# Where a SwiGLU's row scale is multiplied in: on GpSimd onto the gate, or on VectorE onto the up result

## What is computed

```
for l in range(DEPTH):                       # DEPTH = 2
    h = rmsnorm(x, norm_mix[l])
    ... = split(h @ w_in[l])                 # S5, attention, retention -> mix
    x = x + mix @ w_out[l]
    h = rmsnorm(x, norm_ffn[l])              # x * rsqrt(mean(x*x) + eps) * g
    gate, up = split(h @ w_ffn_in[l], 2)     # 2 x 2816 columns
    x = x + (silu(gate) * up) @ w_ffn_out[l]
out = rmsnorm(x, norm_final)
```

## Time and profile before

| what | value |
|---|---|
| median of 3 runs | 2808.41 us (2803.58 to 2812.27) |
| profiled execution: time, span | 2810.1 us, 2808.3 us |
| busy time: PE / DVE / ACT / POOL | 2604.0 / 1568.6 / 1012.6 / 1308.5 us |
| share of the span | 93% / 56% / 36% / 47% |
| mean granted PE clock | 0.963 of full speed |

### The profile page before, as it was taken

How to read it: one execution, slowest core, us unless ns; L and a number is a source line. 1 busy time by engine, 2 the same in 40 slices (tenths; PEclk the granted TensorE clock), 3 DMA queues, 4 the chain that set the end, 5 groups by cost and what they waited for, 6 DMA issues and landing times. The chain is left out here.

```text
span 2808.3 us, 34676 instructions
## 1 busy us (share of the span) xinstructions
PE 2604.0 (93%) x13483; PEld 2058.0 (73%) x13483; DVE 1568.6 (56%) x2785; ACT 1012.6 (36%) x1486; POOL 1308.5 (47%) x818
## 2 busy tenths in 40 slices
PE   7898788989999998899999999988999999999999
PEld 5676555768777786677777777667777777788887
DVE  3858666778999225755231267376898952221112
ACT  5222143424343533232444432342443344322222
POOL 3332143435454474354554442443555446555655
PEclk9989898999999999999999999999999999999999
DMA  5232112212222144222232241221222223433332
GB/s 148 77 120 57 31 31 83 71 57 72 72 78 72 49 154 112 71 68 83 83 89 77 78 134 55 68 60 49 79 76 68 68 61 123 140 91 107 107 109 90
DMA packets 385665, 232.90 MB, mean 83 GB/s; under 512 B 29592, under 2 KB 371552, under 8 KB 383072
## 3 DMA queue, kind: packets, MB, share of 16 engines
q1 hardware_dynamic: 385136, 229.62, 27.6%
q10 hardware_dynamic: 368, 1.08, 0.1%
HBM read 213.88 MB, written 14.69 MB: 81 GB/s over the span
## 5 line engine op out<-in xcount | busy, mean ns | idle before, releaser
L678 POOL TENSOR_TENSOR w_lo<-w_raw,w_hi 128x1024 fp32r<-128x1024 f32 (+2 forms) x408 | 896.2, 2197 | 1353.0 <-ACT w_hi L789 1352.9
L1680 PE MATMUL psum<-h_hi,w_hi 128*128 128x512 f32 x1984 | 804.3, 405 | 32.1 <-POOL w_lo L678 20.3
L789 ACT ACTIVATE w_hi<-w_raw 128x1024 fp32r<-128x1024 f32 (+2 forms) x408 | 397.3, 974 | 1118.3 <-PE psum L1680 1062.3
L1680 PE MATMUL psum<-h_hi,w_lo 128*128 128x512 f32 x1984 | 782.8, 395 | 0.0
L1680 PE MATMUL psum<-h_lo,w_hi 128*128 128x512 f32 x1984 | 769.2, 394 | 0.9 <-POOL h_lo L686 0.9
L1680 PEld LDWEIGHTS psum<-h_hi,w_hi 128*128 128x128 f32 x1984 | 379.7, 191 | 147.2 <-issue 31.2
L1680 PEld LDWEIGHTS psum<-h_hi,w_lo 128*128 128x128 f32 x1984 | 378.6, 191 | 80.7
L1680 PEld LDWEIGHTS psum<-h_lo,w_hi 128*128 128x128 f32 x1984 | 378.9, 191 | 80.0 <-issue 2.5
L1309 DVE MAX8 top<-scores 128x8 f32<-128x512 f32 (+5 forms) x384 | 342.0, 891 | 7.6
L1311 DVE MATCH_REPLACE8 scores<-top,scores 128x512 f32<-128x512 f32 (+5 forms) x384 | 336.3, 876 | 0.0
L1680 PE MATMUL psum<-a_hi,w_hi 128*128 128x512 f32 x704 | 284.8, 404 | 12.4 <-POOL w_lo L678 7.7
(11 more groups left out here) (287 smaller groups left out, 2964.6 us busy)
## 6 DMA issues: line engine op xcount, KB each, us to landing
w_raw<-in_w_ffn_in_dram SPq DMA_DIRECT2D x176, 512.0 KB, 3.8
w_raw<-in_w_ffn_out_dram SPq DMA_DIRECT2D x96, 384.0 KB, 3.5
w_raw<-in_w_in_dram SPq DMA_DIRECT2D x68, 512.0 KB, 3.7
w_raw<-in_w_out_dram SPq DMA_DIRECT2D x32, 512.0 KB, 4.2
x_half<-xs SPq DMA_DIRECT2D x8, 1024.0 KB, 7.1
xs<-x_half SPq DMA_DIRECT2D x8, 1024.0 KB, 7.0
w_raw<-in_w_ffn_out_dram SPq DMA_DIRECT2D x32, 256.0 KB, 2.7
out_dram<-mixed SPq DMA_DIRECT2D x8, 512.0 KB, 3.7
```

Source lines behind the costliest of these rows:

```text
L678: eng.tensor_tensor(w_lo(u, n), w_raw[:, u % 3, 0:n], w_hi[:, u % 2, 0:n].bitcast(F32), ALU.subtract).then_inc(sems["weights_ready"], 1)
L789: act(w_hi[:, u % 2, 0:n], w_raw[:, u % 3, 0:n], ACTF.Copy).then_inc(sems["hi_ready"], 1)
L1680: return eng.matmul(out_, lhsT, rhs, start=start, stop=stop, skip_group_check=True)
```

## The change

On GpSimd the multiplication of `gate` by `row` is gone. On VectorE the eviction of an up bank in a deferred feed-forward becomes two multiplications: the bank times `row` into `atmp`, then `atmp` times `gate` in place. The PSUM bank is free for the next unit after the first one (semaphore `up_scaled`), and the second waits for the first and for the SiLU. The product is the same; the order of its factors is another. The non-deferred feed-forward (0,1) only takes its two waits in another order.

```
@@ gpsimd
                     if kind == "ffn" and i:
                         did, c, f = FFN[i - 1]
-                        if did == "gate" and deferred(kind, l, h):
-                            eng.wait_ge(sems["gate_ready"], st.add("gate_ready"))
-                            eng.tensor_tensor(gate, gate, row, ALU.mult).then_inc(sems["gate_scaled"], 1)
-                        elif did == "gate":
-                            st.add("gate_ready")
@@ vector
                 elif did == "up":
                     eng.wait_ge(sems["unit_done"], u)
-                    st.add("gate_ready")
-                    if later:
-                        eng.wait_ge(sems["gate_scaled"], st.add("gate_scaled"))
-                    else:
-                        eng.wait_ge(sems["gate_ready"], st.now("gate_ready"))
                     if st.now("a_lo_ready"):
                         eng.wait_ge(sems["a_lo_ready"], st.now("a_lo_ready"))
                     st.add("a_lo_ready")
-                    tt(atmp, bank(g), gate, MUL).then_inc(sems["atmp_ready"], 1)
+                    st.add("gate_ready")
+                    if later:
+                        tt(atmp, bank(g), row, MUL).then_inc(sems["up_scaled"], 1)
+                        eng.wait_ge(sems["up_scaled"], st.add("up_scaled"))
+                        eng.wait_ge(sems["gate_ready"], st.now("gate_ready"))
+                        tt(atmp, atmp, gate, MUL).then_inc(sems["atmp_ready"], 1)
+                    else:
+                        eng.wait_ge(sems["gate_ready"], st.now("gate_ready"))
+                        tt(atmp, bank(g), gate, MUL).then_inc(sems["atmp_ready"], 1)
@@ tensor
+                if what != "down" and deferred("ffn", l, h):
+                    st.add("gate_ready" if what == "gate" else "atmp_ready")
                 if what == "gate":
                     unit(g, u, "gated" if deferred("ffn", l, h) else "gate_ready")
                 elif what == "up":
-                    unit(g, u, "atmp_ready")
+                    unit(g, u, "up_scaled" if deferred("ffn", l, h) else "atmp_ready")
```

More of the change, by code:

```diff
@@ L468, in build_trunk @@
                  "tok_ready", "mean_ready", "rstd_ready", "diag_ready", "spread_ready", "norm_tmp", "h_hi_ready",
-                 "h_lo_pool", "h_lo_dve", "k_out", "ik_out", "k_doubled", "ik_doubled", "square_ready", "ssq_added", "sums_ready", "row_ready", "tile_read", "gated", "gate_scaled", "proj_out", "rin_act",
+                 "h_lo_pool", "h_lo_dve", "k_out", "ik_out", "k_doubled", "ik_doubled", "square_ready", "ssq_added", "sums_ready", "row_ready", "tile_read", "gated", "up_scaled", "proj_out", "rin_act",
                  "rin_dve", "vw_turned", "vw_ready", "bias_full", "brow_ready", "bias_stored", "bias_loaded",
```

## The result

The changed kernel takes 2828.85 us (median of 4 runs, 2825.22 to 2832.58) against 2805.99 us for the kernel before (median of 4 runs, 2798.96 to 2812.27; the fourth was made beside the changed kernel): a ratio of 1.0084, with a 95% interval of 1.0063 to 1.0104. It is slower by 23 us (17 to 29 by the interval), where 18.1 were forecast. The profiled execution of the changed kernel took 2826.09 us, with a span of 2824.3 us.

The account below looks back on a forecast made before the run. PE, busy 93% of the span, bounds the kernel, waiting at places for late DVE. Terms sum to 8.8 us in (0,0), 17.6 with (1,0), plus 0.5 for (1,1): 18.1 us slower, 2826.5 us, range 2811 to 2841.

Parts of the forecast that it names:

- POOL's time was worth nothing: POOL's 66 gate scalings, 88.0 us busy, are never waited for by PE, so removing them gains nothing by itself.
- The two gains I put in: In (0,0), PE's wait for the retention's multiplication shrinks by 1.1 us; the copy at 705.91 loses 0.6 or more of waiting.
- Two levels of price: Second multiplication costs DVE 0.73 us if on time, 1.6 to 2.8 if over about 0.4 late, finding w_lo running.
- last up unit: In each deferred feed-forward, the second multiplication holds back the 768-wide w_lo of the following down unit: +0.5 us.
- the two up units before 820: Evictions at 799.55 and 814.44 in (0,0): 0.7 us at the low level, 3.4 at the high; 2.0 taken.
- At 893: Up unit at 893.50 in (0,0), DVE on time: +0.7 us reaches PE at 899.12.
- At 907: Among the other up units in (0,0), where DVE idles behind them for more than they cost: no loss.
- at 670 I followed ACT: Up unit at 670 in (0,0): the late second multiplication delays a_hi, table load, exponential and sum read; PE loses 1.9 us.
- The backlog of 0.6: DVE's remaining backlog from 670, at the next up unit in (0,0): between 0 and 1.2 us, +0.6 taken.
- Only its own 0.73: Rival: the lock is not met, each second multiplication costs only 0.73 us; 4.5 us in all, 2813; chance 0.16.
- DVE becomes the bound: Rival: late evictions meet the lock and make the next late; 32 us in all, 2840; chance 0.06.
- POOL is relieved: Rival: PE's waits for w_lo in the woven halves go, 12.8 us faster, 2796; chance 0.04.

Follow-up runs that it names:

- e1: Kernel before with POOL's scaling of the gate left out and nothing in its place; 2808.45 us, ratio 0.9994.
- e2: Changed kernel with the first product written back into the PSUM bank, where the second multiplication reads it; 2814.77 us, ratio to before 1.0019.
- e9: Kernel before with the change at 56 up units, all but ten late ones in (0,0) and (1,0); 2812.29 us, ratio 1.0020.
- e4: Kernel before with the change in the feed-forward of (1,1) alone; 2810.32 us, ratio 1.0002.
- e8: Kernel before with the change only at ten late up units, five each in (0,0) and (1,0); 2825.05 us, ratio 1.0062.
- e5: Kernel before with the change in the feed-forwards of (0,0) and (1,0) alone; 2831.17 us, ratio 1.0084.
- e3: Changed kernel with POOL waiting for an up unit's second multiplication before it makes the next w_lo; 2814.99 us, ratio to before 1.0023.
- e6: Changed kernel with a third, thrown-away multiplication with two SBUF inputs between the two of each deferred up unit; 2881.84 us, ratio to before 1.0266.

## Why the prediction was right, point by point

**POOL's time was worth nothing.** 75 us left POOL and e1 shows no gain that can be told. Right. The two gains I put in: the retention's wait shrank from 1.51 to 0.41 us:

```profile
527.64 1.21 DVE L1372 TENSOR_TENSOR scratch<-scratch 128x1024 f32<-128x1024 f32 x1
...
528.90 0.33 PE L2016 MATMUL psum<-cst,scratch 128*128 128x128 f32 x1 [0.41 <-DVE scratch L1372]
```

DVE's 2.30 us of the earlier trace rows are 1.21, the rest was waiting. But the 1.1 us did not become time, and this term of the sum was wrong. PE's next 59.04 us (528.90 to 587.94) were 57.41 before (534.91 to 592.32), with a granted clock of 0.94 instead of 0.97, and then PE waits for DVE again: from 520.30 to the DVE result at 607.78 it took 87.48 us before and 87.25 after, in (1,0) 87.33 and 87.30. By the same slower PE the wait for `w_lo` at 599 fell from 3.95 to 2.56 us at no gain: from the wait before it to this one it is 6.93 us in both. e1, e2 and e9 show the 59.0 us too, e4 and e8, where POOL still scales here, the 57.4. Why PE's clock is lower there is not shown. In the copy's stretch PE's two waits stayed (0.97 and 2.04 before, 0.99 and 2.01 after), so the copy's gain and the up unit's price cancelled, as forecast; e1 has the copy's gain alone, 0.34 for 0.97.

**Two levels of price, and the start of `w_lo` between them.** Right. In (1,1) DVE comes first in 21 of 22 places and POOL waits it out, `w_lo` taking 2.54 us instead of 2.40:

```profile
2464.36 0.69 DVE L1264 TENSOR_TENSOR tmp<-psum,tmp 128x512 f32<-128x512 f32 x1 [4.75 <-PE psum L1678]
2465.08 0.69 DVE L1267 TENSOR_TENSOR tmp<-tmp 128x512 f32<-128x512 f32 x1
...
2465.49 2.54 POOL L678 TENSOR_TENSOR w_lo<-w_raw,w_hi 128x1024 fp32r<-128x1024 f32 x1 [3.05 <-ACT w_hi L784]
```

I had forecast 2.7. POOL starts as far behind DVE's eviction as before (1.13 us, 1.14 before) and 0.28 us before the multiplication's end, and only 0.14 of this shows in its duration; why not more is open. I had also said that in (1,1) all would be short: the one at 2486.85 took 1.82 us, beside a `w_lo` 512 wide that starts sooner.

**Place by place in (0,0).** PE's waits in the two timelines, and how long PE took for each stretch, between the same two matmuls (times and stretches of the kernel before):

| stretch, and what is in it | forecast | PE's wait before, after | stretch before, after | change |
|---|---|---|---|---|
| 520 to 608, retention | -1.1 | 1.51, 0.41 | 87.48, 87.25 | -0.2 |
| 608 to 629 | 0 | 0.86, 0.81 | 21.50, 21.48 | 0 |
| 629 to 720, up units at 642 and 670, backlog, copy | +4.4 | 0, 1.87 and 0, 1.69 | 90.48, 94.87 | +4.4 |
| 720 to 743 | 0 | 2.04, 2.01 | 23.32, 23.32 | 0 |
| 743 to 765, up unit at 757 | +1.6 | 0.60, 2.20 | 22.13, 23.56 | +1.4 |
| 765 to 820, up units at 786, 799, 814 | +2.4 | 0, 0.49 and 0.27, 1.00 | 54.85, 57.82 | +3.0 |
| 820 to 847, up unit at 828 | +0.3 | 0, 0.29 | 26.99, 27.27 | +0.3 |
| 847 to 899, up unit at 893 | +0.7 | 0.28, 1.17 | 52.07, 51.74 | -0.3 |
| 899 to 936, up unit at 907 | 0 | 0, 1.10 | 37.05, 38.19 | +1.1 |
| 936 to 987, last up unit | +0.5 | 0.25, 0.59 | 50.57, 51.21 | +0.6 |
| sum | 8.8 | | 466.44, 476.71 | 10.3 |

The sum came near partly by luck: terms were wrong in both directions. (1,0) became 10.5 us longer, between its same two matmuls; with 1.9 in (1,1) that makes 22.7, the 23 of the runs. (The two profiled spans are only 16.0 apart, because in stretches that the change does not touch the changed kernel's execution was 4.9 us shorter before 510 us and 3.4 between the woven halves, and 1.7 longer behind the last feed-forward.)

Besides the retention four terms were mis-sized. For the two up units before 820 I took a value between the levels; by 802 the stall at 765 had made DVE less late against PE, and the low level held: the wait grew by 0.7, not 2.0. At 893 the wait grew by 0.9, but PE had got there faster, at a granted clock of 1.00 instead of 0.94 since 873 us, so that no time was lost. At 907 the long multiplication (2.91 us) did not vanish in DVE's idle time: ACT, whose list is `a_hi` first and then the probabilities' copy L985, waits 3.05 us for it, and PE waits for that copy. I had followed DVE alone there, though at 670 I followed ACT.

The backlog of 0.6 shows in no wait, but from 629 to 720 PE lost 0.8 us more than its waits explain, at a clock of 1.00; I did not settle why. The fourth mis-sized term is one that the prediction lacks: the clock behind the longer wait at 765. The stretch from 765 to 770 us, first after, then before:

```profile
765.00:770.00 5.00, 4.05 (x17) 3.49 (x18) 4.90 (x9) 4.51 (x7) 3.74 (x3) 0.67 0.35 101
```

```profile
765.00:770.00 5.00, 4.73 (x26) 3.98 (x27) 4.90 (x7) 3.84 (x6) 4.42 (x4) 1.00 0.36 107
```

Part of PE's matmuls ran at the lower of the two levels (1.2 GHz) after it had stood for 2.20 us. From 765 to the eviction of the next up unit (772.55 before, 774.77 after) PE fell 1.55 us further behind. The other traces agree: over the 10 us behind this wait the granted clock was 0.83 in the changed kernel, e1, e5 and e8, whose wait was 2.18 to 2.20, and 1.00 in the kernel before, e2, e3 and e9, whose wait was 0.60 to 1.54. Without the waits in it the stretch to 820 took 55.9 to 56.3 us in e1, e8 and the changed kernel, 54.6 to 54.8 in the kernel before, e2 and e9. So the clock cost some 1.5 us here. e1 has no second multiplication, so this term belongs to the wait, whatever makes it long.

A long wait is not always followed by it. (1,0) does not repeat (0,0) exactly: behind its counterpart of the wait at 647 (1.86 us, 1.87 in (0,0)) the granted clock was 0.94 over 29 us, and 1.6 us more were lost than in (0,0), where it was 1.00. At the next late place DVE came after the end of `w_lo`, the second multiplication took 0.69 us, and PE waited 2.91 us, while the stretch grew by only 0.7.

**(1,1).** Forecast +0.5; the profiled executions differ by 1.9 us there, 1.6 of which arise in one stretch, 2513 to 2523 us, with a granted clock of 0.83 that the execution before does not have (1.00). PE waits for `w_lo` in front of it in both, 2.05 and 2.04 us, so the change is not shown to be the cause; e4 puts the change in (1,1) at 0.6 us by its ratio.

**The rivals.** "Only its own 0.73" forecast 4.5 us in all: e2 and e3, where the lock is taken away, measure 5 to 6, so its price was nearly right and its condition false. "DVE becomes the bound" forecast 2840. The sign I gave for it, that the idle time at gate evictions is gone, came true from 675 to 940 us with the change (3.4 us in five places before), but only 7 of 22 second multiplications are long in (0,0) and DVE still waits for PE at some up units, so the sign alone did not decide it. With e6 the time went far beyond. "POOL is relieved" fell with e1.

**PE's new counts.** The hunk on PE also makes it count the gate's evictions of the deferred halves, so that in (0,1) it waits for the right one. No cost shows: through the feed-forward of (0,1), from 1308 us on, every up eviction comes 4.87 or 4.88 us later than in the kernel before.

## What to carry to other kernels

Before an elementwise step is moved between VectorE and GpSimd, look at how many of its inputs lie in SBUF and at what the other engine is doing at that moment: here a VectorE instruction with two SBUF inputs cost 0.69 us or up to 2.9, by whether it started outside or inside an instruction of up to 2.4 us on GpSimd. If it must stay on VectorE, let one input come from PSUM, or make GpSimd wait for it; either took back some 17 of 23 us. Follow a late result through the list of each engine that takes it, the table loads included, since PE may wait for the second one in the row. And don't add up waits alone: a wait that shrinks is time only if the engine reaches the same later instruction sooner, which in e1 and at the retention it hardly did.

## What the runs showed of the hardware that I had not expected

- With one more instruction of this kind in front (e6) the last one took over 2.2 us in 47 of 66 places, in the changed kernel in 4, on an idle VectorE too. It cost 53 us where the 66 added instructions take 46 us alone.
- Behind a wait of PE of 2.2 us the granted clock fell to 0.67 over 5 us and some 1.5 us more were lost; behind waits of 1.5 us at the same place it stayed at 1.00. At another place it fell behind a wait of 2.05 us in one execution and did not behind 2.04 in another.
- In e1 a gain of 1.1 us at one wait of PE was 0.2 us some 70 us later, and the sum over the kernel was not measurable.
